# The last two experts of a mixture-of-experts layer: gate and up weights of both stream ahead of both down weights

## What is computed

```python
g = xblk @ w_gate[e] + b_gate[e]
u = xblk @ w_up[e] + b_up[e]
g = jnp.minimum(g, SWIGLU_LIMIT)
u = jnp.clip(u, -SWIGLU_LIMIT, SWIGLU_LIMIT)
a = (u + 1.0) * (g * jax.nn.sigmoid(SWIGLU_ALPHA * g))
return a @ w_down[e] + b_down[e]
```

## Time and profile before

| | |
|---|---|
| median of 3 runs | 1242.43 us (1241.77 to 1242.64) |
| the profiled execution | 1242.96 us, span in the trace 1241.1 us |
| PE busy | 1198.1 us (97% of the span), mean granted clock 0.996 |
| DVE busy | 492.5 us (40%) |
| ACT busy | 186.7 us (15%) |
| weight DMAs (SP's queue) | 450.55 MB, busy share 87.9% of 16 DMA engines |
| PE matmuls of the products (L914) | 672.8 us in 3056 records |
| bandwidth in the expert part | 425 to 428 GB/s in most slices |

### The profile page before, as it was taken

One profiled execution on the slowest core, in us unless ns is written; L12 is line 12 of the kernel. 1 busy time (PEld: TensorE's weight loads), 2 busy tenths in 40 slices (PEclk: granted clock), 3 DMA queues, 4 the chain that ended last, 5 costly groups with the idle time before them and its releaser, 6 DMA issues.

```text
span 1241.1 us, 15077 instructions
## 1 busy us (share of the span) xinstructions
PE 1198.1 (97%) x5648; PEld 487.8 (39%) x5648; DVE 492.5 (40%) x1189; ACT 186.7 (15%) x394; POOL 10.0 (1%) x13
## 2 busy tenths in 40 slices
PE   8999989999999999999999999999999999999997
PEld 5665654555333333333333333333233333333332
DVE  2399872345432334323332333333343333332323
ACT  3204443133100010100000000000010010010002
POOL 0000000000000000000000000000000000000000
PEclk9999999999999999999999999999999999999999
DMA  9925557829999999999999999999999999999994
GB/s 346 339 80 160 182 189 280 348 91 389 373 393 426 429 425 427 427 428 427 428 427 427 428 428 428 426 427 428 427 426 427 427 426 428 426 425 428 427 425 170
DMA packets 53476, 461.29 MB, mean 372 GB/s; under 512 B 6313, under 2 KB 16361, under 8 KB 27495
## 3 DMA queue, kind: packets, MB, share of 16 engines
q1 hardware_dynamic: 51407, 450.55, 87.9%
q0 software_dynamic: 1152, 8.39, 1.9%
q10 hardware_dynamic: 864, 1.64, 0.4%
HBM read 457.64 MB, written 3.28 MB: 371 GB/s over the span
## 4 chain that ended last, share of the span: by engine, by line
PE 74%; DMA 20%; DVE 4%; issue 1%; ACT 1%; ACTq 0%; SPq 0%; DVEq 0%
PE psum L914 40%; DMA ring<-in_w_up 17%; PE psum L892 6%; PE psum L364 5%; PE psum L956 4%; PE psum L429 3%; DMA ring<-in_w_gate 3%; PE psum L640 2%; DVE ring L1844 2%; PE psum L413 1%; PE psum L768 1%; PE psum L556 1%; PE psum L775 1%; PE psum L600 1%; PE psum L402 1%
## 5 line engine op out<-in xcount | busy, mean ns | idle before, releaser
L914 PE MATMUL psum<-ring,work 128*64 128x512 f32 x3056 | 672.8, 594 | 21.4 <-DMA ring<-in_w_up 20.4
L914 PEld LDWEIGHTS psum<-ring,work 128*64 128x64 f32 x3056 | 214.9, 137 | 468.1 <-issue 413.2
L892 PE MATMUL psum<-H,work 128*64 128x512 f32 (+1 forms) x384 | 92.7, 600 | 0.0
L2281 DVE TENSOR_TENSOR work<-psum,keep 128x512 f32<-128x512 f32 x16 | 11.1, 692 | 158.8 <-PE psum L914 158.8
L1844 DVE SCALAR_TENSOR_TENSOR ring<-ring,extra 128x256 f32<-128x256 f32 x240 | 74.0, 386 | 0.1
L2267 DVE TENSOR_TENSOR X<-X,psum 128x512 f32<-128x512 f32 x63 | 43.2, 686 | 64.6 <-PE psum L956 64.5
L2281 DVE TENSOR_TENSOR work<-psum,work 128x512 f32<-128x512 f32 x16 | 11.1, 692 | 139.9 <-PE psum L914 139.8
L1701 ACT COPY work<-psum 64x512 f32<-64x512 f32 x32 | 18.5, 578 | 296.6 <-PE psum L914 296.6
L1689 ACT COPY work<-psum 128x512 f32<-128x512 f32 x31 | 18.2, 586 | 277.3 <-PE psum L892 277.3
L1680 ACT ACTIVATE work<-work 128x512 f32<-128x512 f32 x32 | 20.1, 629 | 227.8 <-DVE work L2357 227.8
L364 PEld LDWEIGHTS psum<-C,work 128*128 128x128 f32 (+1 forms) x330 | 44.4, 194 | 22.9 <-issue 19.5
(11 more groups left out here) (345 smaller groups left out, 960.7 us busy)
## 6 DMA issues: line engine op xcount, KB each, us to landing
ring<-in_w_gate SPq DMA_DIRECT2D x64, 2048.0 KB, 25.5
ring<-in_w_down SPq DMA_DIRECT2D x63, 2048.0 KB, 29.8
ring<-in_w_up SPq DMA_DIRECT2D x61, 2048.0 KB, 28.4
ring<-in_cache_keys SPq DMA_DIRECT2D x64, 144.0 KB, 3.0
ring<-in_w_in SPq DMA_DIRECT2D x1, 4096.0 KB, 25.8
ring<-in_mem_keys_turned SPq DMA_DIRECT2D x8, 512.0 KB, 14.1
ring<-in_cache_mem_v SPq DMA_DIRECT2D x8, 512.0 KB, 7.5
ring<-in_w_in SPq DMA_DIRECT2D x1, 2688.0 KB, 19.4
```

The source lines that it names most:

```text
L892: last = mm(psum[64 * nh:64 * nh + 64, 2, :], Ph[0:ROWS[tt], tt, :], xn[0:ROWS[tt], tt, 512 * nh:512 * nh + 512], start=tt == 0, stop=tt == 2)
L914: last = mm(psum[64 * nh:64 * nh + 64, bank, :], src[:, j, 64 * half:64 * half + 64], w[:, j, 512 * nh:512 * nh + 512], start=first and j ...
L2281: v.tensor_tensor(gm, psum[:, 0, :], B[b][:, 0:512], ALU.add).then_inc(s.g_sum, 1)
```

## The change

The order in which the last group's matrices stream changes by a table, `LAST_ORDER`: matrices are numbered 3q + t in a group (t is 0 for gate, 1 for up, 2 for down), so 6, 7, 8 are expert 30's and 9, 10, 11 expert 31's. Number 8 now comes after 10. `at_half` and SP's `refills` follow the table. On the PE, expert 30 returns before its down product (`hold_down`), and expert 31 does that product after its own up product, one half before the turn of its activation and one half after. Expert 31's down product now goes to bank 1, and ACT copies expert 30's result in expert 31's turn. DVE's `AT` copy of expert 31 waits until expert 30's down product has read `AT`. The split DMAs are now the two halves of the last down matrix (1/2 + 1/2, then 3/4 + 1/4); the last up matrix has none. The bias rows of expert 31 are issued between the halves of its gate matrix, and no longer ahead of both.

```diff
+LAST_ORDER = (0, 1, 2, 3, 4, 5, 6, 7, 9, 10, 8, 11)
...
+            if isinstance(i, int) and i == NE // 4 - 1 and u < 24:
+                u = 2 * LAST_ORDER.index(u // 2) + u % 2
             return (u - 1) % 8, i * 3 + (u + 7) // 8
...
             def product(bank, src, pos, half, first, last_half, end=None, early=None):
                 w = v3(held(pos), D)
                 for j in range(4):
-                    if end and j == 3:
-                        pe.wait_ge(*end)
+                    if end and j == end[2]:
+                        pe.wait_ge(end[0], end[1])
...
-                        last = product(t, XT[q % 2], pos, half, half == 0, half == 1,
-                                       (s.part_up, 32) if last_one and t and half else None,
+                        last = product(t, XT[q % 2], pos, half, half == 0, half == 1, None,
                                        s.first_rows if first and t == 0 and half == 0 else None)
...
-                        if last_one and t == 0 and half == 0:
-                            sums_begin(0, 0)
+                        if last_one and (t == 0 or half == 0):
+                            sums_begin(t, half)
                     if t == 0:
-                        pe.wait_ge(s.y_moved, e + 1)
+                        if not last_one:
+                            pe.wait_ge(s.y_moved, e + 1)
...
-                        if last_one:
-                            sums_begin(0, 1)
...
                 if last_one:
-                    sums_begin(1, 0)
+                    pe.wait_ge(s.pgt_moved, pairs + 2)
                     sums_begin(1, 1)
+                    down_before(0)
                 else:
                     scatter_pair(1 + 2 * (q % 2), q // 2 + 1, pairs * 5)
...
                 if last_one:
+                    down_before(1)
                     sample_begin()
                 else:
                     scatter_pair(2 + 2 * (q % 2), q // 2 + 1, pairs * 5)
...
+                if hold_down:
+                    return
                 pe.wait_ge(s.at_moved, e + 1)
                 m = 3 * q + 2
                 for half in range(2):
                     pos, n = at_half(i, 2 * m + half)
                     pe.wait_ge(ring_in[pos], n * 16)
-                    product(2, AT, pos, half, half == 0, half == 1,
-                            (s.end_down, 16) if last_one and half else None).then_inc(ring_used[pos], 1)
+                    product(1 if last_one else 2, AT, pos, half, half == 0, half == 1,
+                            ((s.part_up, 32, 2), (s.end_down, 16, 3))[half] if last_one else None).then_inc(ring_used[pos], 1)
+
+            def down_before(half):
+
+                pe.wait_ge(s.at_moved, NE - 1)
+                pe.wait_ge(s.y_moved, NE - 1)
+                pos, n = at_half(NE // 4 - 1, 16 + half)
+                pe.wait_ge(ring_in[pos], n * 16)
+                product(2, AT, pos, half, half == 0, half == 1).then_inc(ring_used[pos], 1)
...
-                expert(NE // 4 - 1, q, last_one=q == 3)
+                expert(NE // 4 - 1, q, hold_down=q == 2, last_one=q == 3)
...
-                    if m % 3 == 0 and half == 0:
+                    if m % 3 == 0 and half == (last_one and m == 9):
                         sp.wait_ge(s.u_clip, i * 4 + m // 3)
                         load_bias((m // 3) % 2, e)
-                    if last_one and half:
-                        load_end(pos, src[1], s.part_up if m % 3 == 1 else s.end_down)
+                    if last_one and m == 11:
+                        load_end(pos, src[half], (s.part_up, s.end_down)[half], 2 + half)
...
+                rows = {}
+                for m in range(4, 4 + count) if count == 12 else LAST_ORDER[4:]:
...
+                if last_one:
+                    used(act, i, 3 * q - 1)
+                    nc.scalar.copy(Y[1][0][0:64, :], psum[0:64, 2, :])
+                    nc.scalar.copy(Y[1][1][0:64, :], psum[64:128, 2, :]).then_inc(s.y_moved, 1)
...
                 dve.wait_ge(s.at_full, e + 1)
-                dve.wait_ge(s.y_moved, e + 1)
+                if last_one:
+                    used(dve, i, 3 * q - 1)
+                else:
+                    dve.wait_ge(s.y_moved, e + 1)
                 v.tensor_copy(AT, v3(psum[:, 4, :], 128)).then_inc(s.at_moved, 1)
```

More of the change, by code:

```diff
@@ L1074, in scatter_again, with expert @@
                 last.then_inc(s.ov_sc, 1)
-            def expert(i, q, first=False, since=None, last_one=False):
+            def expert(i, q, first=False, since=None, hold_down=False, last_one=False):
                 e, pairs = i * 4 + q, i * 2 + q // 2
@@ L1310, in load_half, with load_end @@
                 dma(held(pos), src).then_inc(ring_in[pos], 16)
-            def load_end(pos, src, end):
-                dma(held(pos)[:, 0:3 * D], src[:, 0:3 * D]).then_inc(ring_in[pos], 16)
-                dma(held(pos)[:, 3 * D:], src[:, 3 * D:]).then_inc(end, 16)
+            def load_end(pos, src, end, j):
+                dma(held(pos)[:, 0:j * D], src[:, 0:j * D]).then_inc(ring_in[pos], 16)
+                dma(held(pos)[:, j * D:], src[:, j * D:]).then_inc(end, 16)
             def load_whole(m):
@@ L1338, in _, with refill @@
             load_half(8, weights(1, 1)[0])
-            def refill(l, i, e, last_one=False):
-                m = 4 + l
+            def refill(m, i, e, last_one=False):
                 src = weights(m % 3, e)
@@ L1363, in refills @@
             def refills(i, count):
-                for l in range(count):
-                    if l == 0 or (4 + l) % 3 == 0:
-                        at = i * 4 + (4 + l) // 3
+                rows = {}
+                for m in range(4, 4 + count) if count == 12 else LAST_ORDER[4:]:
+                    if m // 3 not in rows:
+                        at = i * 4 + m // 3
                         at = slice(at, at + 1) if isinstance(at, int) else bass.ds(at, 1)
-                        e = sp.value_load(order[0:1, at], min_val=0, max_val=NE - 1)
-                    refill(l, i, e, count < 12 and l >= 6)
+                        rows[m // 3] = sp.value_load(order[0:1, at], min_val=0, max_val=NE - 1)
+                    refill(m, i, rows[m // 3], count < 12)
             sp.wait_ge(s.y_moved, 1)
@@ L1674, in _, with expert @@
             nc.scalar.copy(PgT[1][0:NE, :], psum[0:NE, 5, 0:T]).then_inc(s.pgt_moved, 1)
-            def expert(i, q, twice=False, last_one=False):
+            def expert(i, q, twice=False, hold_down=False, last_one=False):
                 e = i * 4 + q
@@ L1700, in expert @@
                 lo = 64 * (q % 2)
-                last = nc.scalar.copy(Y[q // 2][0][lo:lo + 64, :], psum[0:64, 2, :])
+                last = nc.scalar.copy(Y[q // 2][0][lo:lo + 64, :], psum[0:64, 1 if last_one else 2, :])
                 if not last_one:
@@ L2397, in expert @@
                     used(dve, i, m)
-                    v.tensor_copy(Y[q // 2][1][64:128, :], psum[64:128, 2, :]).then_inc(s.y_last, 1)
+                    v.tensor_copy(Y[q // 2][1][64:128, :], psum[64:128, 1, :]).then_inc(s.y_last, 1)
                 else:
```

## The result

The changed kernel took 1248.4 us (median of 13 runs, 1243.08 to 1250.9), the kernel before beside it 1242.24 us (13 runs, 1240.89 to 1250.91). The ratio estimated over all the runs is 1.0037, 95% interval 1.0021 to 1.0053: slower, by 0.37% (the two medians by themselves are 0.50% apart). I had forecast 1244.8 and a range up to 1246.4.

A forecast was written before the change was run, and what follows sets the result against it. It took the PE's gapless work behind expert 30's last up landing as the bound; token wait 1.51, cuts 0.74 and `AT` copy 0.08 sum to 2.33 us, giving a median of 1244.8 us, range 1243.0 to 1246.4.

The forecast's parts named there:

- The last stretch: From expert 30's second up half landing at 1184.39 us to the last product: 44.2 us of gapless PE work, becoming 46.5.
- the token wait: Before expert 31's first gate half, PE idles for DVE's `move_tokens`: 1.51 us (1.3 to 1.7); rival without it 1243.3, chance 0.10.
- The cuts: Seven product blocks instead of four, separated sum calls and a turn between products on the PE: 0.74 us, bounds 0 to 1.2.
- `AT` copy: DVE's copy for expert 31 must wait for expert 30's down product, sticking out past the sample part: 0.08 us, at most 0.99.
- Single calls: A residual sum of one call behind a product takes 1.05 us, against 0.86 inside a row of calls.
- blocks of one half: A PE product block of one half takes 3.59 us; each new block costs 0.15.
- the turn between two products: Turn of expert 31's activation, now between products: 0.66 us, 0.10 more than behind sum calls.
- the sample part with the copy behind it: Before expert 31's down product: `AT` copy path of 0.99 us over a sample part of 0.91.
- No new wait for data: In the last stretch every weight half lands 5 us or more before its new time of use.
- `g_final` harmless: Last load on SP's queue, landing 6.3 us after issue; rival that it delays the last weights: 1247.6, chance 0.08.
- The step from the profiled execution to the median: Profiled execution, 1242.96 us before and 1245.3 after, lay 0.53 above the median, so the median becomes 1244.8.
- the two cases: Slower (0.43) and within 0.2% of before (0.52); the line between them at 1244.9 us, inside the forecast's range.

The follow-up runs named there:

- whole blocks: Tokens first, plus the third residual sum put back beside the fourth and expert 30's down product in one block ahead of the turn: median 1242.83 us, ratio 1.0004.
- tokens first: Changed kernel, but DVE scales expert 31's tokens before adding expert 30's last scatter piece: median 1242.94 us, ratio 0.9997; on another chip median 1244.73.

## Why the prediction was wrong

**The last stretch: right.** That the PE's work behind 1184.4 us bounds the end, that the reorder can't shorten it, and that the gate product would wait for `move_tokens` is what the profile after shows. The terms: the token wait, forecast at 1.51 us, made the stretch up to the first gate matmul 1.64 longer (1195.26 - 1183.80 against 1194.21 - 1184.39, where the next product began before), and took 1.5 by itself in the old order. The cuts and the `AT` copy, forecast at 0.74 + 0.08, came to 0.93 (35.32 us against 34.39 from there on). Single calls took 1.06 and blocks of one half 3.58, as forecast; the turn between two products took 0.68 and not 0.66; the sample part with the copy behind it took 1.04 and not 0.99. Sum 2.57 against 2.33. That the profiled execution came out so near, 1244.95 against 1245.3, is in part luck: expert 30's up matrix happened to land 0.59 us earlier (1183.80 against 1184.39), which more than makes up for the 0.24 missing from the sum. The prices of the cuts and of the `AT` copy were confirmed by whole blocks: 0.30 + 0.19 + 0.08 by the prediction's prices, 0.57 measured.

**No new wait for data, `g_final` harmless: right.** The last quarter landed 39.5 us behind the end of the up wait, before (1223.85 - 1184.35) and after (1188.03 + 35.2 - 1183.75). `g_final`, issued at 1214.14, took 10.3 us and not 6.3, to 1224.4: it came behind the weights and did not hold them up.

**The step from the profiled execution to the median: wrong.** I wrote that the profiled execution "lay 0.53 above the median of the runs" and so "the median becomes 1244.8", as if the times of this kernel were one cluster some tenths of a us wide. They are two clusters 6 us apart. With three runs of before, all in the lower one, I took their spread for the spread of the kernel, and gave no rival to a second level. The forecast holds for the lower group (1244.4 and 1244.6 in the first two sets of runs). The median is 1248.4 because 7 of 13 runs fell in the upper group; where 5 or 4 of 12 did, it is 1245.4 and 1245.6, inside the range. With shares so near one half, chance has a part in which group holds the median. No term of the sum for the last stretch makes these 6 us: they arise at 118 to 131 us, and the distance at the end is 46.8 in both groups. Whether the change makes them more frequent is the question left open above. The profile of before shows the PE's wait of 0.99 us at 116 us, and I did not read that part of it, since the change is elsewhere.

**The chances.** I gave 0.43 to slower and 0.52 to within 0.2%. The lower groups differ by 2.2 us in two sets (1244.4 and 1242.2; 1244.6 and 1242.3) and by 3.2 in the third (1244.9 and 1241.7), 0.18 to 0.25%, so the line between the two cases ran through the forecast, as said. The upper group tipped it.

## What to carry to other kernels

Before reordering a stream, see whether anyone waits for it in the stretch where the order changes; here the PE had 44 us of work without a gap behind its last wait, and in these runs the order gained something only where the PE waited. See too how near the engine is to waiting: at expert 31's up matrix it came 1.4 us behind the landing, so that moving the sums away from in front of it brought a wait back. A product moved forward takes its own inputs' waits with it: look what the old neighbour was hiding. And before a change of some tenths of a per cent is judged, look at the whole list of times for two levels: an idle time of 1 us far from the change can decide by a coin's throw over 6 us, and four idle-filling matmuls were worth more than the change that was studied.

## What the runs showed of the hardware

- Behind an idle time of 0.99 us of the PE, in a stretch of small matmuls, the granted clock fell to 0.50 for 13.7 us in all six traces of the upper group and in none of ten others without the filling; by the times, 25 of 107 executions of the kernel before and 18 of 41 of the changed one belong to that group. With that time filled no mean clock of 24 was below 0.995. The fall began 2.1 to 2.8 us (by the windows' shares) behind the end of the idle time, while the PE was turning queries. Behind an idle time of 1.6 us ahead of product matmuls (64 columns by 512) it never fell in eight traces; behind one of 4.5 us it fell for 3.4 us in the one trace.
- 13.7 us at half the clock cost about 6.0 us between the groups' medians, over a thousand us later, nearly all of the 6.9 us that the PE lost: the stream of expert weights, whose first load is issued at 210 us, never made that up. In the five such traces of the changed kernel and of tokens first, the wait for expert 30's up matrix ended 4.7 to 5.4 us later than in the changed kernel's first profile.
- Filling 1 us of idle time with matmuls cost nothing in the times: the lower groups with and without it are 1242.2 and 1241.7 (before), 1244.4 and 1244.9 (changed).
